# Moving TensorE's operands to other byte offsets: a two-block transformer kernel on one Trainium2 core

## What is computed

```python
def reference(x, ...):
    x = first_block(x, ...)      # FFN (swiglu, 2816 wide), neighbourhood + dilated attention, FFN
    return second_block(x, ...)  # 2 layers: w_in (7168 columns), recurrence + attention + Fourier,
                                 # merge, w_out, then square(relu(h @ w1)) @ w2, 4096 wide

def swiglu(x, w_gate, w_up, w_down):
    return (jax.nn.silu(x @ w_gate) * (x @ w_up)) @ w_down
def sq_relu_mlp(h, w1, w2):
    return jnp.square(jax.nn.relu(h @ w1)) @ w2
```

## Time and profile before

| | |
|---|---|
| median of 3 runs | 1942.03 us (1940.7 to 1943.5) |
| the profiled execution: its time, its span | 1941.69 us, 1939.7 us |
| PE busy | 1889.4 us (97%), 12606 matmuls |
| PE weight loads | 1668.0 us (86%), 12606 |
| DVE, ACT, POOL busy | 63%, 49%, 24% |
| HBM read | 294.02 MB, 153 GB/s over the span |
| TensorE's granted clock | full (2.4 GHz) in nearly all of the span |

### The profile page before, as it was taken

The page is one execution under the profiler, slowest core; times in us unless marked ns, Lnnn a source line. Parts: engine busy times, 40 slices in busy tenths (PEclk is TensorE's granted clock), DMA queues, the critical chain, the costliest instruction groups (busy, mean ns, idle before and its releaser), DMA issues.

```text
span 1939.7 us, 31204 instructions
## 1 busy us (share of the span) xinstructions
PE 1889.4 (97%) x12606; PEld 1668.0 (86%) x12606; DVE 1229.7 (63%) x1975; ACT 944.8 (49%) x1508; POOL 475.1 (24%) x328
## 2 busy tenths in 40 slices
PE   8999999999999999999999999999999899999999
PEld 8989988999988887777788888888898898799988
DVE  6888898779856943666663743354376947776410
ACT  6444446655456443426733531233265554765643
POOL 2211022000000000003344354555500000304887
PEclk9999999999999999999999999999999999999999
DMA  8987663567733112221123354466632343154554
GB/s 300 272 255 260 198 226 129 178 226 237 272 119 100 64 55 87 87 66 44 66 98 130 109 163 141 153 216 210 178 102 98 117 132 123 65 174 146 182 194 152
DMA packets 83951, 297.12 MB, mean 153 GB/s; under 512 B 9704, under 2 KB 12912, under 8 KB 83552
## 3 DMA queue, kind: packets, MB, share of 16 engines
q1 hardware_dynamic: 65600, 232.81, 36.4%
q0 software_dynamic: 16592, 58.79, 10.0%
q10 hardware_dynamic: 1616, 3.52, 0.5%
HBM read 294.02 MB, written 2.54 MB: 153 GB/s over the span
## 4 chain that ended last, share of the span: by engine, by line
PE 78%; DVE 11%; ACT 4%; issue 3%; DMA 2%; POOL 1%; DVEq 0%; SPq 0%; ACTq 0%; POOLq 0%
PE ps L598 20%; PE ps L593 20%; PE ps L596 20%; DVE wl L461 4%; PE ps L590 3%; DMA wr<-wstream 2%; ACT wh L445 2%; PE ps L592 1%; PE ps L1277 1%; PE ps L1381 1%; PE ps L1282 1%; PE ps L1279 1%; PE ps L1421 1%; PE ps L2162 1%; PE ps L1400 1%
## 5 line engine op out<-in xcount | busy, mean ns | idle before, releaser
L593 PE MATMUL ps<-HH,wh 128*128 128x256 f32 (+1 forms) x2160 | 703.4, 326 | 1.3 <-DVE K L2428 0.9
L598 PE MATMUL ps<-HH,wl 128*128 128x256 f32 (+1 forms) x2160 | 691.6, 320 | 12.1 <-DVE wl L461 9.9
L596 PE MATMUL ps<-HL,wh 128*128 128x256 f32 (+1 forms) x2160 | 690.0, 319 | 0.0
L445 ACT ACTIVATE wh<-wr 128x1024 fp32r<-128x1024 f32 x440 | 459.2, 1052 | 331.0 <-PE ps L598 231.0
L461 DVE TENSOR_TENSOR wl<-wr,wh 128x1024 fp32r<-128x1024 f32 x301 | 366.4, 1221 | 188.2 <-ACT wh L445 187.4
L598 PEld LDWEIGHTS ps<-HH,wl 128*128 128x128 f32 x2160 | 406.9, 188 | 47.1 <-DVE wl L461 13.7
L593 PEld LDWEIGHTS ps<-HH,wh 128*128 128x128 f32 x2160 | 407.2, 189 | 41.7 <-issue 6.6
L596 PEld LDWEIGHTS ps<-HL,wh 128*128 128x128 f32 x2160 | 407.3, 189 | 33.3 <-issue 2.4
L461 POOL TENSOR_TENSOR wl<-wr,wh 128x1024 fp32r<-128x1024 f32 x139 | 337.3, 2429 | 211.9 <-ACT wh L445 205.3
L1536 POOL TENSOR_TENSOR s<-s,ST 128x512 f32<-128x512 f32 x56 | 57.3, 1040 | 665.2 <-DVE ST L1504 665.0
L1134 DVE CUSTOM_DVE_ANT_0 PROD<-WM,COND 128x1024 f32<-128x1024 f32 x104 | 129.8, 1261 | 1.3
(11 more groups left out here) (312 smaller groups left out, 2967.6 us busy)
## 6 DMA issues: line engine op xcount, KB each, us to landing
wr<-wstream SPq DMA_DIRECT2D x440, 512.0 KB, 3.4
WM<-wmod POOLq DMA_DIRECT2D x68, 512.0 KB, 4.5
X<-wmod POOLq DMA_DIRECT2D x28, 512.0 KB, 6.6
NAB<-naskew POOLq DMA_DIRECT2D x16, 128.0 KB, 7.5
DILB<-dilskew POOLq DMA_DIRECT2D x8, 256.0 KB, 8.2
COND<-cond ACTq DMA_DIRECT2D x2, 1024.0 KB, 4.6
X<-xin SPq DMA_DIRECT2D x4, 256.0 KB, 5.5
HL<-cond ACTq DMA_DIRECT2D x1, 1024.0 KB, 7.8
```

What stands on the lines that cost most here:

```text
L445: ins = e.activation(self.WH[i % NSPL][:, :], self.WR[n % NRAW][:, :], ACT.Copy)
L593: e.matmul(out, wh, xh, start=i == 0, stop=False)
L596: e.matmul(out, wh, xl, start=False, stop=False)
L598: return e.matmul(out, wl, xh, start=False, stop=i == n_k - 1)
```

## The change

Only places in SBUF move; the instructions, their number, their order on each engine and their waits are the same. In detail:

- wh0, wh1, wh2 move to 32, 64 and 96 modulo 128, and wl0, wl1, wl2 likewise, with 128 modulo 256 between a wh and its wl.
- LINE goes from 64 to 128. HH's and HL's rows become 544 float32 (2176 bytes, a multiple of 128) instead of 528 (2112 bytes, which is 64 modulo 128). The wide form starts at 0 modulo 128 in every row, the short ones at 96 (first block) and 32 (layer 1).
- The arena's base is 64 modulo 128 (0 before); tensors made with `past` stand at 96 (32 before), HID1 at 0 (32 before).
- tm, rm and the constants CT move along with the linear allocation (64 to 0 modulo 128).

```diff
-LINE, PAST = 64, 32
+LINE, PAST = 128, 32
 ROW = 512 + LINE // 4
...
-        self.WH = [sb(f"wh{i}", [128, 1024], F32R) for i in range(NSPL)]
-        self.WL = [sb(f"wl{i}", [128, 1024], F32R) for i in range(NSPL)]
+        split_at, each = (nc.sbuf_base + LINE - 1) // LINE * LINE, 4096 + 32
+        self.WH, self.WL = ([nc.alloc_sbuf_tensor_at(f"{n}{i}", [128, 1024], F32R,
+                                                     offset=split_at + half * (3 * each + 32) + i * each + 32)
+                             for i in range(NSPL)] for half, n in enumerate(("wh", "wl")))
+        sb("split", [128, (2 * (3 * each + 32) + LINE) // 4])
...
-        self.short_halves = [[x[:, :, n:n + 256] for x in halves] for n in (4, 2)]
+        self.short_halves = [[x[:, :, n:n + 256] for x in halves] for n in (24, 8)]
...
-        base = (nc.sbuf_base + LINE - 1) // LINE * LINE
+        base = (nc.sbuf_base + LINE - 1) // LINE * LINE + 64
...
-        hidden1 = past("HID1", 0, [2, 32, 256], F32R)
+        hidden1 = at_("HID1", 64 / KB_, [2, 32, 256], F32R)
```

## The result

| | before | after |
|---|---|---|
| median, measured side by side (20 runs each) | 1941.45 us | 1944.63 us (1942.0 to 1949.2) |
| ratio, 95% interval | | 1.0020 [1.0014, 1.0026] |
| profiled execution: time, span | 1941.69, 1939.7 us | 1946.53, 1944.6 us |
| first to last matmul, start to start | 1929.3 us | 1934.5 us |

The change makes the kernel 3 us slower. The forecast was 1939.9 us, 2 us faster. The time lies in the wide range (1927 to 1953) and 0.6 us outside the levelling case's own (1936 to 1944); the sign is wrong.

A forecast was written before the change was run, and what follows sets the result against it. The prediction took PE to bound the kernel, through matmul count times start-to-start distance. Its terms summed to -2.1 us, from the median basis of 1942.0 to 1939.9 us, with 8 in 10 between 1927 and 1953 us.

The forecast's parts named there:

- levelling case: All stages: good fixed phases lose, bad ones win, rotation makes a mean; 1936 to 1944 us, chance 0.47.
- Part 6: Arena tensors at 512 columns, 984 matmuls: leave equal phase, 226.7 to 230.5 ns, +3.7 us.
- Part 1: Short HH, first block, some 2690 matmuls: 118.9 to some 117.9 ns, -2.7 us.
- Part 5: Wide HH at 512 columns with turned stages, 2544 matmuls: 232.1 to 231.4 ns, -1.8 us.
- Part 2: Short HH, layer 1, 960 matmuls: 120.0 to 117.9 ns, -2.0 us.
- Part 3: Y1 and other arena tensors at 256 columns, some 430 matmuls: 120.0 to 117.9 ns, -0.9 us.
- Part 4: NHH/NHL, 1056 matmuls: leave the best phase seen, 116.7 to 117.9 ns, +1.3 us.
- Part 7: HID1, 224 pairs and 96 at 256 columns: from the 32-byte phase to a mixture, some +0.3 us.
- Part 8: Wide HH at 256 columns, some 1250 matmuls: a mixture stays a mixture, 0.
- Spread phases win: Rival: rarely coinciding phases give 116.7 and 228.7 ns everywhere; -18.9 us, 1923 us, chance 0.27.
- Slower: the mixture is worse: Rival: phase jumps between wh and wl; 120 ns at 256, 232 or 233 at 512; +17.6 us, 1959.6 us, chance 0.19.
- Nothing: Rival: ports are independent, today's differences come from something else; 1942.0 us, chance 0.07.

The follow-up runs named there:

- e10: Kernel before with only the arena's base 32 bytes further, so HIDH at relation 32; 1946.81 us in one execution, beside 1939.76 for the kernel before.
- e7: Kernel before with only the six weights' halves 32 bytes further; 1950.68 us in one execution, 11 us slower than before.
- e11: Changed kernel with all six weights' halves at 192 modulo 256, the arena's place; 1935.87 us, ratio to before 0.9970.
- e3: Kernel before with only the six weights' buffers spread as in the change; 1947.66 us, ratio to before 1.0037.
- e2: Changed kernel with all six weights' halves at 128 modulo 256; 1945.49 us, ratio 1.0025.
- e1: Changed kernel with each wl at the same place modulo 256 as its wh; 1944.67 us, ratio to before 1.0023.
- e5: Kernel before with all weights at 160 modulo 256, rows of 2304 bytes and one relation in each stage; 1926.85 us, ratio to before 0.9929.
- e6: e5 with everything from the weights on 32 bytes lower, all relations kept; 1925.43 us, ratio 0.9924.
- e9: e6 with PAST 192 in place of 64, so NHH and NHL stand at relation 192; 1925.78 us, ratio 0.9919.

## Why the prediction failed, step by step

- **PE is the bound, and only the distances can change the time:** right. The length of the two-input rows stayed (686 and 685 ns), PE's idle time before the low halves' product too.
- **Part 6, the arena at 512 columns, one of the two steps that failed:** mis-sized by 1.9 us. It took 228.7 ns for HIDH at relation 32, read from HID1, and a mixture of 230.5. HIDH is at 233.3 there (e10) and at 224 (e7), so the mixture came to 232.4 and the term to +5.6 us, just beyond its own upper bound of +5.3. HID1's matmul takes its 512 columns from two tensors; its order of relations is another one (best at 32, worse at 0), so its row was no price for HIDH's. The other bound was the mean of wide HH, 232.1, and a mean is no upper bound of a single relation.
- **Part 1, short HH of the first block, the other step that failed:** mis-sized by 2.2 us, more than part 6. The 118.9 ns of the earlier trace rows came from 27 matmuls, where start times printed to 0.01 us leave 0.4 ns open; the stage's mean is 118.4. The gain was 0.2 ns a matmul and not 1.0.
- **Part 5:** the direction was right (231.5), the size 0.5 ns where 0.7 was taken, and the turned stages went the other way. The part of the gain that was to be had by a smaller change is seen in e11 (230.2).
- **Parts 2, 3, 4 and 7:** right to 0.4 us each. Part 2's gain arrived in the distances; in the profiled execution most of it was used up by the fall of the clock after the wait for POOL.
- **Part 8:** taken as 0, was +0.8: a mixture did not stay a mixture.
- **Levelling as the mechanism:** right. Stages at a good fixed relation (HIDH, NHH) lost, stages at a bad one (short HH of layer 1, Y1) won, and no stage left the bounds of 116.7 to 120 and 226.7 to 233 in its mean. With part 6 at +5.6 and part 1 at -0.5 the forecast's own sum is +2.0, the measured sign; with only one of them put right it is -0.2 or +0.1, so neither decided the sign alone. e3 and e11 show what the spreading costs: 7 us on the kernel before, and 9 on the rest of the change against weights at the arena's place, 5.6 of them in the arena's 512-column matmuls. But e2 is as slow without any spreading. What loses is that the heaviest stages leave relation 0; the spreading is one way to do that.
- **The rivals.** "Spread phases win" failed on the same value as part 6, since it priced relation 32 at 228.7 everywhere. "Slower: the mixture is worse" had a mechanism that exists (e1: a block at relation 0 has 227.1 ns without the jump and 231.3 with it) but on one buffer of three. Its 232 to 233 for the arena is what was measured, its 120 at 256 columns is not (117.8 to 118.4). "Nothing" is refuted by e7 and e10, 11 and 7 us for 32 bytes of relation.
- **Ports.** The Trainium skill's rule from "SBUF — State Buffer", "Who interferes with whom", that the ports for the moving operand and the weights are independent, would give e7 and e10 the time of before. The traces disagree: 233.3 against 226.7 ns for the same matmuls.

## What to carry to other kernels

Where PE is the bound, read the distance from matmul to matmul of each stage, and set it beside the difference of the two operands' addresses modulo 256; give each stage one relation that the trace shows to be good (here 0 at 512 columns, 192 at 256), with rows and buffers that are multiples of 256 bytes apart. Spreading buffers so that they don't coincide makes a mean of good and bad, and costs when the heaviest stages already stood well. Price a step by a row of the same shape and the same kind of operand, over a whole stage, and never by a stretch of 27 matmuls or by the mean of a mixture.

## What the runs showed that I had not expected

- At 512 columns HIDH's distance goes with the relation alone, in two levels with one between: 226.7 ns at 0, 228.9 at 64, 233.3 at 32, 192 and 224. That is 3% of a stage for 32 bytes. HID1 doesn't keep to this: at relation 64 it had 233.6 in e10 and 230.0 in e11. Nor does wide HH where its rows alternate: in e2 the rows at relation 0 have 233.1 ns and those at 128 between them 231.0, while with every row at 0 it is 227.3 (e5). So a row's price depends on its neighbours' too, and a mixture can't be priced as the mean of its relations.
- At 256 columns one relation can hold two steady paces: 117.7 and 113.3 ns at relation 192 (e6 and e9, the same instructions and relations). In the changed kernel's NHH one block on wh0 took 113.8 ns a matmul and the next block on wh0 118.8:

```profile
501.90 0.28 PE L596 MATMUL ps<-NHH,wh 128*128 128x256 f32 x1
...
504.63 0.28 PE L596 MATMUL ps<-NHH,wh 128*128 128x256 f32 x1
...
510.34 0.28 PE L596 MATMUL ps<-NHH,wh 128*128 128x256 f32 x1
...
513.19 0.28 PE L596 MATMUL ps<-NHH,wh 128*128 128x256 f32 x1
```

  (2.73 / 24 and 2.85 / 24.) What picks the pace was not found. In e9 the quick one set in right behind the stretch at half the clock, but it also ran in e6, which had no such stretch. A run that starts a stage in a controlled way would be needed.
- A wait of 1.93 us for POOL's low half in layer 1 is followed by some 3 us at 0.50 of the clock in seven of the thirteen traces, and by none in the others, before and e1 among them, where the wait is as long. The first feed-forward has such a fall in e5, e9 and e10; in the trace of the kernel before a wait of 2.25 us at 119.9 us brought none.
- Of the 19.6 us that e5 wins in distances, 5.8 come back, about half of them as idle time of PE. At 1926 us the making of the weights' halves may be the next thing to look at; no run tried it. The shortest steady distances seen, 226.7 and 113.3 ns, are 6% over 512 and 256 columns at 2.4 GHz (213.3 and 106.7).
- The Trainium skill, "TensorE: Matmul & The Clock Gate", section "Wait — 56ns, not 53.3ns?", gives the distance at the full clock as columns / 2.4 GHz plus some 2.5 ns, measured on bf16 matmuls; worked out for these widths that is an estimate of 215.8 and 109.2 ns. No stage of any of these traces, in rounded float32 with weights loaded for each matmul, comes that low.
